# The recurrence of a two-block model: masks by kind, two turned copies on VectorE, other places for key roots, bonus, convolution taps and norm

## What is computed

```python
u = u * sigmoid(u_gate);  u = causal_dwconv(u, w, b)        # 31 taps, 512 channels
u = silu(layer_norm(u) * conv_ln_g + conv_ln_b)
r, k, v, wd, ad, gd = split(p_rw + (prev - p_rw) * mu)
decay = exp(-exp(w_log(w0 + tanh(wd) @ w2)));  a = sigmoid(a0 + ad @ a2);  g = sigmoid(gd) @ g2
kk = k * k_k;  kk = kk / max(norm(kk), 1e-12);  k = k * (1 + (a - 1) * k_a)
def step(S, inp):                                           # one token
    s_kk = einsum('bhij,bhj->bhi', S, kk_t)
    S = S * w_t - s_kk * (a_t * kk_t) + v_t * k_t
    return S, einsum('bhij,bhj->bhi', S, r_t)
y = (layer_norm(y) * lnx_g + lnx_b + sum(r * k * r_k) * v) * g
out = concat([u, y]) @ w_out
```

## Time and profile before

| | us |
|---|---|
| median of 3 runs | 1838.8 (1838.51 to 1844.3) |
| the profiled execution, its own time | 1840.75 |
| its span | 1839.0 |
| busy in the span: PE, PEld | 1737.6, 1414.5 |
| busy in the span: POOL, DVE, ACT | 1020.7, 968.3, 366.9 |
| mean granted clock of TensorE | 0.97 |

### The profile page before, as it was taken

The page is one execution under the profiler, slowest core; times in us unless marked ns, Lnnn a source line. Parts: engine busy times, 40 slices in busy tenths (PEclk is TensorE's granted clock), DMA queues, the critical chain, the costliest instruction groups (busy, mean ns, idle before and its releaser), DMA issues.

```text
span 1839.0 us, 27586 instructions
## 1 busy us (share of the span) xinstructions
PE 1737.6 (94%) x10626; PEld 1414.5 (77%) x10626; DVE 968.3 (53%) x1381; ACT 366.9 (20%) x632; POOL 1020.7 (56%) x598
## 2 busy tenths in 40 slices
PE   5999999999999989999999899977889899999996
PEld 4888888878775678888888767866777788888885
DVE  6555652323266357555552449965655666676113
ACT  3000000011045321111101121323332233332000
POOL 4876667755456567666677544620003266666674
PEclk9999999999999999999999889988989799999998
DMA  4443443232220034444433222200001033232332
GB/s 168 149 144 141 139 147 115 103 108 81 76 70 1 2 107 149 149 137 152 144 138 110 85 69 81 92 24 2 3 2 69 23 103 103 91 102 92 103 108 99
DMA packets 48801, 173.82 MB, mean 95 GB/s; under 512 B 5424, under 2 KB 5808, under 8 KB 48464
## 3 DMA queue, kind: packets, MB, share of 16 engines
q1 hardware_dynamic: 39888, 143.00, 22.5%
q10 hardware_dynamic: 8832, 29.63, 4.7%
HBM read 170.51 MB, written 2.10 MB: 94 GB/s over the span
## 4 chain that ended last, share of the span: by engine, by line
PE 89%; DVE 6%; ACT 2%; issue 2%; POOL 1%; DMA 0%; SPq 0%; DVEq 0%; ACTq 0%; POOLq 0%
PE banks L456 25%; PE banks L457 24%; PE banks L458 24%; PE banks L850 4%; PE banks L502 2%; PE banks L752 1%; PE banks L738 1%; PE banks L515 1%; DVE in_arena L1873 1%; PE banks L825 1%; DVE h_lo L1531 1%; POOL prob L430 1%; PE banks L495 1%; PE banks L718 1%; DVE tmp L1488 0%
## 5 line engine op out<-in xcount | busy, mean ns | idle before, releaser
L421 POOL TENSOR_SCALAR w_hi<-w_raw 128x1024 fp32r<-128x1024 f32 x264 | 299.7, 1135 | 740.0 <-DMA w_raw<-in_slabs 739.7
L423 POOL TENSOR_TENSOR w_lo<-w_raw,w_hi 128x1024 fp32r<-128x1024 f32 x264 | 652.0, 2470 | 22.0
L456 PE MATMUL banks<-h_hi,w_hi 128*128 128x512 f32 x1464 | 581.4, 397 | 27.4 <-DVE h_lo L1531 20.9
L457 PE MATMUL banks<-h_lo,w_hi 128*128 128x512 f32 x1464 | 575.2, 393 | 0.0
L458 PE MATMUL banks<-h_hi,w_lo 128*128 128x512 f32 x1464 | 574.9, 393 | 0.0
L456 PEld LDWEIGHTS banks<-h_hi,w_hi 128*128 128x128 f32 x1464 | 278.4, 190 | 93.3 <-issue 29.8
L458 PEld LDWEIGHTS banks<-h_hi,w_lo 128*128 128x128 f32 x1464 | 278.1, 190 | 59.3
L457 PEld LDWEIGHTS banks<-h_lo,w_hi 128*128 128x128 f32 x1464 | 278.5, 190 | 58.3 <-issue 1.2
L456 PE MATMUL banks<-act_hi,w_hi 128*128 128x512 f32 x528 | 205.4, 389 | 0.0
L457 PE MATMUL banks<-act_lo,w_hi 128*128 128x512 f32 x528 | 205.4, 389 | 0.0
L458 PE MATMUL banks<-act_hi,w_lo 128*128 128x512 f32 x528 | 205.4, 389 | 0.0
(11 more groups left out here) (297 smaller groups left out, 1716.6 us busy)
## 6 DMA issues: line engine op xcount, KB each, us to landing
w_raw<-in_slabs SPq DMA_DIRECT2D x264, 512.0 KB, 3.2
adaw<-in_ada ACTq DMA_DIRECT2D x48, 512.0 KB, 3.4
xT<-in_x SPq DMA_DIRECT2D x2, 1024.0 KB, 7.0
relb<-in_relb ACTq DMA_DIRECT2D x8, 256.0 KB, 2.8
out_y<-xT SPq DMA_DIRECT2D x8, 256.0 KB, 2.0
block<-in_block ACTq DMA_DIRECT2D x1, 704.0 KB, 4.4
silc<-in_ada ACTq DMA_DIRECT2D x1, 512.0 KB, 3.7
tmp<-in_rope ACTq DMA_DIRECT2D x1, 512.0 KB, 3.4
```

Source lines behind the costliest of these rows:

```text
L421: nc.gpsimd.tensor_scalar(w_hi[:, r, :], w_raw[:, r, :], 1.0, 1.0, ALU.mult, ALU.mult).then_inc(S("w_hi"), 1)
L423: nc.gpsimd.tensor_tensor(w_lo[:, r, :], w_raw[:, r, :], w_hi[:, r, :], ALU.subtract).then_inc(S("w_split"), 1)
L456: mm(out, hi, rhs_hi, start=start, stop=False, skip_group_check=True)
L457: mm(out, hi, rhs_lo, start=False, stop=False, skip_group_check=True)
```

## The change

Nothing is computed in another way; the order on three engines and the place of three buffers differ.

- VectorE does 68 taps instead of 62 by the end of the fourth gate and six fewer behind the shifts of input slabs 18 to 20; `factors(0, g)` comes one slab earlier.
- VectorE moves tk and tb. Masks come by kind: ar, p0 of both groups, mr, mt of both, q0 of both, then r0 of both.
- Half 0: ScalarE moves q2 first, then the decays of group 0, q3, and only then the key roots. `bonus_sum(1, g)` goes behind level 1 and level 2; its operands lie in `conv_gate` and `g2b`, so the decays wait for nothing of it. Taps: 4 ahead of r3 and 4 behind r5, where 6 stood ahead of r3.
- Half 1: taps 6, 4, 3 and, behind r3, 3, where there were 4, 4 and 10 ahead of r3. `out(0)` goes from behind r3 to behind r4. `conv_mean` goes behind level 2, `conv_stats` behind rho, `conv_spread` behind hd; the squares, root and reciprocal follow.

```diff
@@ -226,7 +226,7 @@
         mixed_of = [[mQ[:, g, :] for g in range(2)], [lora_act[:, g, :] for g in range(2)]]
-        bonus_of = [[mR[:, g, :] for g in range(2)], [lora[:, g, :] for g in range(2)]]
+        bonus_of = [[mR[:, g, :] for g in range(2)], [conv_gate[:, 0, :], g2b_t[:, :]]]
@@ -967,8 +967,6 @@
                     made([(mQ, mR)], by_token, by_token, "r3", g, half)
-                if half == 0:
-                    bonus_sum(1, 0)
@@ -982,12 +980,10 @@
                             made([(mP, mQ)], by_feature, by_token, "r4" if lvl == 1 else "r5", g, half, across)
-                    if half and lvl == 1:
-                        conv_mean()
-                if half == 0:
-                    bonus_sum(1, 1)
-                else:
-                    conv_stats()
+                    if half == 0:
+                        bonus_sum(1, lvl - 1)
+                if half:
+                    conv_mean()
@@ -999,10 +995,12 @@
                 if half:
-                    conv_spread()
+                    conv_stats()
...
                         made([(tokK, tokV), (tokB, mZ)], by_token, by_feature, "hd", g, half, across)
+                if half:
+                    conv_spread()
@@ -1082,8 +1080,8 @@
                 project(m)
-                if m in (4, 5, 6):
-                    lora_products(4 * (m - 4), 4 * (m - 4) + 4)
+                if m in (5, 6, 7):
+                    lora_products(4 * (m - 5), 4 * (m - 5) + 4)
@@ -1340,8 +1338,6 @@
                 act.wait_ge(S("rk_bz"), 2 * half + g + 1)
-                if half:
-                    act.wait_ge(S("rk_bsum"), 2 + g + 1)
@@ -1350,8 +1346,6 @@
                 for g in range(2):
-                    move("tk", tokK, g, half)
-                    move("tb", tokB, g, half, scale=-1.0)
@@ -1365,28 +1359,22 @@
                     key_square_of(1, 1)
-                    key_rs(1)
...
                     move("q2", mQ, g, half)
+                if half == 0:
+                    decays(1, 0)
...
                 else:
-                    decays(1, 0)
+                    key_rs(1)
...
                         move(f"y{lvl}", mQ, g, half)
-                    if half and lvl == 1:
-                        for j in range(4):
-                            act.wait_ge(S("conv_d"), j + 1)
-                            f(conv_square[j], conv_out[:, j, :], ACT.Square).then_inc(S("conv_square"), 1)
-                    elif half:
-                        act.wait_ge(S("conv_stat"), 4)
-                        f(n_std, bank[7][:, 0:4], ACT.Sqrt, bias=1e-5, scale=1.0 / 512).then_inc(S("conv_std"), 1)
@@ -1394,6 +1382,11 @@
                     for j in range(4):
+                        act.wait_ge(S("conv_d"), j + 1)
+                        f(conv_square[j], conv_out[:, j, :], ACT.Square).then_inc(S("conv_square"), 1)
+                    act.wait_ge(S("conv_stat"), 4)
+                    f(n_std, bank[7][:, 0:4], ACT.Sqrt, bias=1e-5, scale=1.0 / 512).then_inc(S("conv_std"), 1)
+                    for j in range(4):
@@ -1419,15 +1412,14 @@
                 raw_in(m)
-            gate_in(0)
...
             f(lora_act2[0:32, :], lora_act2[0:32, :], ACT.Sigmoid).then_inc(S("lora_act"), 1)
+            gate_in(0)
             lora_outs(0, 4)
-            lora_outs(4, 8)
             gate_in(1)
-            lora_outs(8, 12)
+            lora_outs(4, 12)
@@ -1895,11 +1887,12 @@
                 for g in range(2):
-
+                    move("tk", half, g, lambda b: v.tensor_copy(rows(tokK, g), b))
+                    move("tb", half, g, lambda b: v.tensor_scalar(rows(tokB, g), b, -1.0, None, ALU.mult))
+                for g in range(2):
...
                     move("p0", half, g, lambda b: masked(mP, b, "np0", g))
-                    dve.wait_ge(S("rk_p0"), n0 + g + 1)
-                    v.tensor_tensor(rows(mR, g), rows(mP, g), every_chunk(const("eye64")), ALU.add).then_inc(S("rk_r0"), 1)
+                for g in range(2):
@@ -1908,12 +1901,15 @@
                     masked(mQ, b, "nq0", g).then_inc(S("rk_q0"), 1)
+                for g in range(2):
+                    dve.wait_ge(S("rk_p0"), n0 + g + 1)
+                    v.tensor_tensor(rows(mR, g), rows(mP, g), every_chunk(const("eye64")), ALU.add).then_inc(S("rk_r0"), 1)
...
                 else:
-                    convolve(4)
+                    convolve(6)
@@ -1931,45 +1927,47 @@
                     add_r("r2", g)
-                convolve_to(len(taps) if half else taps_in2 + 6)
+                convolve(3 if half else 4)
...
                 if half:
-                    out(0)
+                    convolve_to(len(taps))
...
                     factors(1, 0)
-                    bonus(1, 0)
...
                         add_r("r4" if lvl == 1 else "r5", g, ALU.subtract)
-                    if half == 0:
-                        if lvl == 1:
-                            prepare(1, 1)
+                    if half == 0 and lvl == 1:
+                        prepare(1, 1)
+                    elif half == 0:
+                        bonus(1, 0)
+                        convolve(4)
                     elif lvl == 1:
+                        out(0)
+                    else:
...
                                 .then_inc(S("conv_d"), 1)
-                    else:
-                        dve.wait_ge(S("conv_std"), 1)
-                        v.reciprocal(n_rs, n_std).then_inc(S("conv_rs"), 1)
...
                     move("rho", half, g, lambda b: v.tensor_tensor(rows(r_, g), rows(r_, g), b, ALU.add))
+                for g in range(2):
+                    de = d_end[half][:, 8 * g:8 * g + 8].unsqueeze(2).to_broadcast([P, NC, CH])
+                    move("hd", half, g, lambda b: v.tensor_tensor(rows(mHD, g), b, de, ALU.mult))
                 if half:
+                    dve.wait_ge(S("conv_std"), 1)
+                    v.reciprocal(n_rs, n_std).then_inc(S("conv_rs"), 1)
...
                                                in1=bank[6][:, :], op0=ALU.mult, op1=ALU.mult).then_inc(S("conv_t"), 1)
-                for g in range(2):
-                    de = d_end[half][:, 8 * g:8 * g + 8].unsqueeze(2).to_broadcast([P, NC, CH])
-                    move("hd", half, g, lambda b: v.tensor_tensor(rows(mHD, g), b, de, ALU.mult))
-                if half == 0:
+                else:
@@ -2008,7 +2006,7 @@
                     .then_inc(S("conv_in"), 1)
-                convolve_to((14, 40, 62, 62)[j])
+                convolve_to((14, 40, 62, 68)[j])
@@ -2021,9 +2019,9 @@
                     keys(1, m - 10)
-                if m in (12, 13):
-                    factors(0, m - 12)
-                convolve((5, 4, 5, 2, 2, 4, 5, 4, 4, 2, 1, 0)[m - 3])
+                if m in (11, 12):
+                    factors(0, m - 11)
+                convolve((5, 4, 5, 2, 2, 4, 5, 2, 1, 1, 1, 0)[m - 3])
...
```

## The result

The changed kernel takes 1813.35 us, the median of 4 runs (1808.74 to 1815.01), and the kernel before 1840.81 (median of 4 runs, 1838.51 to 1844.3): a ratio of 0.9845, with a 95% interval of 0.9819 to 0.9872. The forecast was 1802.5 us with a range of 1796 to 1815. The sign and the range held; the gain is 27.5 us where 36.4 were forecast. The forecast's own spread ended at 1811; the range reached 1815 only because the time of rival A was taken into it.

The account below looks back on a forecast made before the run. TensorE, busy 94% of the span, was taken as the bound, with 32 us of waits and a 0.90 clock in the recurrence. Terms summed to 38.4 us, less 2 for clock drops: 36.4, so 1802.5 us against the median, range 1796 to 1815.

Parts of the forecast that it names:

- rival A: Input's stage: VectorE ends it where it ended before, its operations stretched by GpSimd; 12 us less gain, 1814.5 us, chance 0.11.
- the clock, as a reserve: Lower clock behind the four short pauses left in the recurrence: 2 us taken of a possible 7.8.
- Terms 2 to 5: Masks and turned copies, 2.0+1.6+1.6+0.4 us; half 0's key roots, 6.3+1.3, and bonus and levels, 4.8; half 1's last taps, 5.4.
- term 6: Half 1, mean, sums and spread moved: 6.1 us gained from rt1 to z, 1.7 behind it, minus 5.7 after rho.
- term 4: Half 0, bonus and levels, from r3's end to z: 20.1 us become 15.3, a gain of 4.8.
- term 1: Input's stage: products one slab later, tanh ahead of the gate, six taps earlier: 10.3 us, and 2.6 in the transposes.
- rival B: Recurrence: the clock follows the pauses, four drops and hd at full price; 7 us less gain, 1809.5; within the forecast's 0.80.
- Rivals C and D: C: waits return elsewhere, nothing changes, 1838.8 us, chance 0.04; D: TensorE stays at 1.2 GHz through the recurrence, 1844, 0.05.

## Where the prediction was right and where it was wrong

The terms, in the order of the prediction, as differences between the trace of before and the one of the changed kernel, each counted between the same two instructions:

| term | forecast | measured |
|---|---|---|
| 1, input's stage, to the first transpose | 10.3 | 6.4 |
| 1, the eight transposes | 2.6 | 0.3 |
| 2, q1 in half 0 (11.88 to 9.97) | 2.0 | 1.9 |
| 2, the 128 records (5.50 to 3.95) | 1.6 | 1.6 |
| 2, q1 in half 1 (12.0 to 9.97) | 1.6 | 2.0 |
| 2, tk and tb, the start of half 1 (24.2 to 25.1) | 0.4 | -0.9 |
| 3, r1 to r3's end (19.06 to 11.58), forecast as 6.3 + 1.3 | 7.6 | 7.5 |
| 4, r3's end to z (20.1 to 15.0) | 4.8 | 5.1 |
| 5, r3's end to rt1 in half 1 (6.87 to 1.35) | 5.4 | 5.5 |
| 6, rt1 to z (21.4 to 15.5) | 6.1 | 5.9 |
| 6, z's 80 records (6.25 to 4.58) | 1.7 | 1.7 |
| 6, rho's end to the first state step | -5.7 | -6.5 |
| sum | 38.4 | 30.5 |
| the clock, as a reserve | -2.0 | in the terms |

The table rests on one trace of each kernel, and a single row can be off by the clock of that execution.

**What was right.** Terms 2 to 5 and the first two parts of term 6, in which a wait that a row shows by name was taken away: 30.8 us were forecast in them (without tk and tb) and 31.2 measured, none off by more than 0.4. One of these hits is in part luck: the 1.6 us of the 128 records was forecast for a pause of at most 1.6 us and came behind one of 2.18, behind which the clock fell in four of twelve traces. Three of them were put back one at a time. From the anchor to the state step they cost 7.8 us (roots), 6.5 (masks) and 8.0 (half 1's order), where they had brought 7.5, 4.6 and 6.6 by the table; by the medians 6 to 7, 4.6 and 3.5 to 4.6. So each is shown to bring time, and its size to one or two us at best. Of the pauses that were to be left, those ahead of rt1 are 1.35 us in half 1 and 1.22 in half 0 (1.45 forecast) and the one ahead of the spread 0.87 (1.0); the one ahead of q1 in half 0 is 2.18, more than the 1.6 at most that I gave it. The roots fitted behind q3: they end at 1244.4 and rt1's move begins at 1244.31, without a gap. In half 1 the gap of 0.41 us in the earlier trace rows is gone, as tk and tb on VectorE were to bring.

```profile
1242.05 1.28 ACT L1314 ACT_TABLE_LOAD   x1
1243.34 1.07 ACT L1314 ACTIVATE banks<-banks 128x512 f32<-128x512 f32 x2
1244.31 2.07 ACT L1306 ACTIVATE in_arena<-banks 128x512 f32<-128x512 f32 x4
```

A table load takes 1.28 us here and the root's operation begins 0.01 us behind its end. The prediction had weighed this against the figure of the Trainium skill, page "ScalarE: Activation LUTs", section "What ACT_TABLE_LOAD costs", about 2.66 us a switch with the drain. By that figure, as an estimate, rt1 would have been moved some 2.8 us later. The trace doesn't agree: term 4 came out 0.3 us better than forecast, so the trace's value was the right one.

The extra table load of term 1 did lie in ScalarE's idle time: tanh's load begins at 1071.39 us, the one for the sigmoids at 1073.34, and the gate's operation follows at 1081.58 behind 5.79 us of idle time. The reason given for it ahead of the prediction, that tanh stands in another table than the sigmoids, is not the whole of it. In the trace of before, tanh (1079.68) ran right behind the gate's sigmoid (1079.19) with no load between them, so it stands in the sigmoids' table as well; run first, it is given another.

**What the prediction had named as its own signs.** The roots, the wait ahead of r2, rt1 in half 1, the order of the tail, the wait of the spread and the clock of 0.95 came as it said. Two signs did not: the first transpose was to stand near 1198 and stood at 1204.48, later than the 1202 from which it called itself wrong (at 1202.0 if the later anchor is taken off), and the eight transposes were to take under 4.5 us and took 6.24. Both belong to term 1. The tail took 14.8 us, just under its limit of 15.

**The step that failed** is in term 1: "So its end moves by 6.5 + 4.0 = 10.5". TensorE's 6.5 us came: the last slab's copy on ScalarE, 1203.02 before, is at 1199.06 now, 6.4 earlier from the anchor. The taps' 4.0 didn't. That step took VectorE's work for a fixed sum of durations, into whose idle time six taps can be moved. The idle time did shrink, by 10.8 us (19.4 to 8.7). But what an operation takes depended on whether POOL's instruction was running as it began, and once the stage was dense, more of them met one, 13 instead of 8: VectorE's busy time for the same 146 operations rose by 4.5 us. The runs with POOL's subtraction left out and with the taps taken back show both sides of this. It was rival A by its mechanism and half its price: it put 12 us on it, and 3.9 in the stage with 2.3 in the transposes came, 6.2. That the time, 1813.35, lies so near rival A's 1814.5 is luck: the rest of the distance is other misses and the later start of the stretch. I had held against it that POOL has as many slabs to split as before; it is not the count that matters, but how many operations meet them.

**The transposes** were forecast at 3.9 us on a pause of 1.5; the pause stayed at 5.46, and the term hung on the first one. The rows for it: 6.24 us behind 5.46, 3.71 behind 1.57, in the kernel with the products back 5.38 behind 1.99. The pause alone doesn't set the time: behind pauses of 5.39 to 5.57 us the eight traces that have one, that of before among them, show 5.02 to 6.56. The windows of the changed kernel around the pause, in steps of 4 us:

```profile
1200.00:1204.00 4.00, 0.00 (x0) 0.00 (x0) 4.00 (x8) 0.00 (x0) 1.36 (x2) 0.86 0.41 131
1204.00:1208.00 4.00, 3.52 (x17) 3.53 (x18) 1.09 (x2) 1.20 (x2) 2.04 (x1) 0.50 0.02 4
1208.00:1212.00 4.00, 4.00 (x41) 3.83 (x41) 2.01 (x4) 1.20 (x2) 0.00 (x0) 0.79 0.00 0
```

TensorE does nothing in the first of them, and 0.50 (1.2 GHz) is granted in the second.

**Smaller misses.** From rho's end the prediction counted to the first state step of all, 7.6 us before; the table counts to the first one that waits for VectorE, 8.3 before, and does so for both kernels. The start of half 1 came 0.9 us later and not 0.4 earlier. VectorE and ScalarE were as fast as reckoned, but TensorE's end of half 0's y took 2.83 us and the transposes 4.27, at a clock of 0.82 and 0.76, where the kernel with the reciprocal first had 1.85 and 3.88 on the same code; in the second trace of the changed kernel they took as long, 2.82 and 4.29. In the tail, hd stands behind the sums, in windows with a clock of 0.80 and 0.77, and takes 5.4 us where I had put 4.5. The factor of z's records was the right row but not the whole of it. Both belong to rival B, which had 7 us for all such places together; with the transposes' 2.3, already counted above, the 1.3 here and hd's 0.9 it came to about 4.5, against the 2 that I had set aside.

**The sum.** From the forecast's 38.4 the misses are the stage (3.9), the transposes (2.3), the start of half 1 (1.3) and the tail (0.8), and all other rows together came out 0.4 better: 38.4 - 3.9 - 2.3 - 1.3 - 0.8 + 0.4 = 30.5. Against the 36.4 forecast that leaves 5.9 us. The medians differ by 27.5, so another 3 us of the miss lie outside what these two traces show of the stretch, and these runs don't explain them. Rivals C and D didn't come: none of the waits turned up again elsewhere, and the mean clock over the recurrence rose from 0.90 to 0.95.

## What to carry to other kernels

Where GpSimd reads SBUF beside VectorE, VectorE's work is not a sum of durations: count how many of its operations with only SBUF operands begin under a GpSimd instruction, and move out of the crowded stage altogether what can be moved, instead of packing it denser. The taps with an operand in PSUM were not held up here, so such a stage is best filled with their like. And before two executions are compared stage by stage, choose an anchor ahead of the change, and take the scatter of the distances from more than two traces: the anchor wandered by 5.5 us here, and the distances from it by 0.1 to 2.2 us, depending on how much of TensorE's clock lies between.

## What I had not expected of the hardware

- A copy of eight columns, 0.16 us by itself, took 2.34 us beside POOL's subtraction and ended 0.03 us behind it: the delay goes by what is left of POOL's instruction, not by the size of VectorE's.
- POOL's own subtraction, 2.46 us in the mean of the whole run, took 3.17 us in one of these rows and 2.7 in two, where VectorE's operations met it.
- The sums, 32 matmuls with one column each, take 3.73 us at a granted clock of 1.00, up to 5.06 where it falls during them and 6.98 at 0.50; the matmuls behind them took longer in every order that was tried. What in the sums brings it about these runs don't show.
- The pause of 1.35 us in the second half of the changed kernel cost no clock. One of 1.99 us ahead of the transposes went with a low clock (5.38 us for eight), one of 1.57 with the full one (3.71). Behind pauses of 5.39 to 5.57 us, the same eight took anything from 5.02 to 6.56 us. The pause of 2.18 us ahead of q1 in half 0 left the 128 records at 3.95 us in eight traces and went with 5.45 to 5.50 in four. What decides between them these runs don't show.
